# PEER channel mixer: another order for the low halves, the one-hot pairs and the packed operands on VectorE and ScalarE

## The reference

```python
q = (xb @ w_q).reshape(P_BLOCK, P_HEADS, P_QDIM)
s1, s2 = q[..., :128] @ k1.T, q[..., 128:] @ k2.T      # 128 keys each
v1, i1 = lax.top_k(s1, 16);  v2, i2 = lax.top_k(s2, 16)
cand = v1[..., :, None] + v2[..., None, :]
top_s, pos = lax.top_k(cand, 16)                       # 16 of 256 pairs, 8 heads
eid = take(i1 * 128 + i2, pos);  gate = softmax(top_s)
act = gelu(einsum(u_tab[eid], xb))                     # exact GELU
out = einsum(gate * act, v_tab[eid])
```

## Time and profile before

| | us |
|---|---|
| runs, median of 3 | 1959.04 |
| profiled execution, its own time | 1959.04 |
| its span, first to last instruction | 1957.3 |
| TensorE busy | 1925.2 (98%) |
| VectorE busy | 1430.1 (73%) |
| ScalarE busy | 1183.5 (60%) |
| GpSimd busy | 237.9 (12%) |
| mean granted TensorE clock | 0.999 of full speed |

### The profile page before, as it was taken

One profiled execution on the slowest core, in us unless ns is written; L12 is line 12 of the kernel. 1 busy time (PEld: TensorE's weight loads), 2 busy tenths in 40 slices (PEclk: granted clock), 3 DMA queues, 4 the chain that ended last, 5 costly groups with the idle time before them and its releaser, 6 DMA issues.

```text
span 1957.3 us, 40098 instructions
## 1 busy us (share of the span) xinstructions
PE 1925.2 (98%) x13148; PEld 1747.0 (89%) x13148; DVE 1430.1 (73%) x2525; ACT 1183.5 (60%) x1610; POOL 237.9 (12%) x106
## 2 busy tenths in 40 slices
PE   8989999999999999999999999999999999999998
PEld 6878999999999888888888799999999998888887
DVE  4775896889898666666658669868989876666666
ACT  4534446888887455555565544568888865555554
POOL 0113743000000000000006067310000000000000
PEclk9999999999999999999999999999999999999999
DMA  7744455444445555555554345554444455555554
GB/s 250 244 139 158 157 191 174 151 150 150 153 152 164 197 193 193 193 193 192 193 162 139 129 148 167 180 167 154 153 150 150 152 182 193 193 193 193 193 193 150
DMA packets 92817, 338.97 MB, mean 173 GB/s; under 512 B 10384, under 2 KB 10512, under 8 KB 92240
## 3 DMA queue, kind: packets, MB, share of 16 engines
q1 hardware_dynamic: 90864, 329.49, 51.3%
q0 software_dynamic: 1888, 8.62, 1.4%
HBM read 337.02 MB, written 1.05 MB: 173 GB/s over the span
## 4 chain that ended last, share of the span: by engine, by line
PE 88%; issue 3%; DVE 3%; POOL 3%; ACT 1%; DMA 0%; SPq 0%; POOLq 0%; DVEq 0%; ACTq 0%
PE psum L1132 88%; POOL tile_lo L386 3%; DVE tile_lo L726 1%; ACT tile_hi L457 1%; DMA raw<-in_a_in 0%; DVE zv L827 0%; DVE qe L1070 0%; DVE zu L836 0%; DVE ke L1071 0%; ACT hT_hi L492 0%; DVE zu L801 0%; DVE hn L776 0%; DVE score_in L1082 0%; DVE x L760 0%; DVE yT_lo L842 0%
## 5 line engine op out<-in xcount | busy, mean ns | idle before, releaser
L726 DVE TENSOR_TENSOR tile_lo<-raw,tile_hi 128x1024 fp32r<-128x1024 f32 x564 | 696.2, 1234 | 282.7 <-ACT tile_hi L457 282.3
L457 ACT ACTIVATE tile_hi<-raw 128x1024 fp32r<-128x1024 f32 x624 | 655.8, 1052 | 270.6 <-PE psum L1132 268.2
L1132 PE MATMUL psum<-hT_hi,tile_hi 128*128 128x256 f32 x2368 | 595.6, 290 | 3.4 <-ACT hT_hi L492 2.7
L1132 PE MATMUL psum<-hT_lo,tile_hi 128*128 128x256 f32 x2368 | 577.6, 283 | 0.0
L1132 PEld LDWEIGHTS psum<-hT_hi,tile_hi 128*128 128x128 f32 x2368 | 451.2, 191 | 7.9 <-ACT hT_hi L492 3.4
L1132 PEld LDWEIGHTS psum<-hT_lo,tile_hi 128*128 128x128 f32 x2368 | 452.3, 192 | 0.0
L1132 PE MATMUL psum<-hT_hi,tile_lo 128*128 128x256 f32 x2368 | 332.1, 283 | 0.5 <-POOL tile_lo L386 0.5
L597 ACT ACTIVATE w_hi<-acts 128x256 fp32r (+1 forms) x256 | 106.7, 418 | 340.8 <-PE psum L1132 340.8
L1132 PEld LDWEIGHTS psum<-hT_hi,tile_lo 128*128 128x128 f32 x2368 | 305.4, 192 | 1.2 <-POOL tile_lo L386 0.9
L1132 PE MATMUL psum<-tile_lo,w_hi 128*128 128x512 f32 x1024 | 274.9, 389 | 0.0
L1132 PE MATMUL psum<-tile_hi,w_lo 128*128 128x512 f32 x1024 | 274.7, 389 | 0.0
(11 more groups left out here) (194 smaller groups left out, 1479.3 us busy)
## 6 DMA issues: line engine op xcount, KB each, us to landing
raw<-in_u SPq DMA_DIRECT2D x256, 512.0 KB, 3.4
raw<-in_v SPq DMA_DIRECT2D x256, 512.0 KB, 3.4
raw<-in_a_in SPq DMA_DIRECT2D x32, 512.0 KB, 4.7
raw<-in_w_q SPq DMA_DIRECT2D x32, 512.0 KB, 3.4
raw<-in_a_out SPq DMA_DIRECT2D x16, 512.0 KB, 3.4
raw<-in_b_rv SPq DMA_DIRECT2D x16, 512.0 KB, 3.4
raw<-in_b_qk SPq DMA_DIRECT2D x8, 512.0 KB, 3.4
raw<-in_b_out SPq DMA_DIRECT2D x8, 512.0 KB, 3.4
```

The lines of the kernel that those rows point to most:

```text
L457: act.activation(tile_hi[slot % SPLIT_SLOTS][:, :], raw[slot][:, :], ACT.Copy).then_inc(hi_ready, 1)
L726: dve.tensor_tensor(tile_lo[s][:, :], raw[slot][:, :], tile_hi[s][:, :].bitcast(F32), ALU.subtract).then_inc(lo_ready, 1)
L1132: return pe.matmul(o, a, b, start=start, stop=stop, skip_group_check=True)
```

## The change

The lookup on VectorE writes its lower halves at other places; the one-hot pairs of the first two groups begin later and only two groups are packed before the late tiles; in each late tile VectorE runs the gate, the one-hot pair, the lower half, the product and then the weighting, where it ran pair, gate, weighting, lower half and product; and ScalarE packs group g + 2 in the tile of group g and waits for the weighted copies before both of its two instructions.

```diff
@@ ScalarE
-                def pack_group(slot, hot, ready, used):
-                    act.wait_ge(hot_ready[l], hot)
+                def pack_group(slot, ready, used):
+                    act.wait_ge(weighted_ready[l], ready)
                     if used is not None:
                         act.wait_ge(gmat_done[l], used)
                     act.activation(pack[:, slot, 0, ...], hot_a ...)
-                    act.wait_ge(weighted_ready[l], ready)
                     act.activation(pack[:, slot, 1:4, ...], weighted ...)
...
-                early_tiles(EARLY - 4, EARLY - 2)
-                pack_group(0, 1, 1, None)
-                early_tiles(EARLY - 2, EARLY - 1)
-                pack_group(1, 3, 2, None)
-                early_tiles(EARLY - 1, EARLY)
+                early_tiles(EARLY - 4, EARLY - 3)
+                pack_group(0, 1, None)
+                early_tiles(EARLY - 3, EARLY - 2)
+                pack_group(1, 2, None)
+                early_tiles(EARLY - 2, EARLY)
                 act.wait_ge(w16_ready[l], 1)
-                pack_group(0, 5, 3, 1)
...
-                    if more:
-                        g = next_group(c) + 2
+                    if more and c in GROUP_AT:
+                        g = GROUP_AT.index(c) + 2
@@ VectorE, lookup
                 n = UT[l] + POOL_U
+                lo_at(n)
...
+                lo_at(n + 1)
+                n += 2
...
                         d2 = did(dve.tensor_tensor(look ... ALU.mult))
-                        lo_at(n)
-                        n += 1
+                        if h == 0:
+                            lo_at(n)
+                            n += 1
...
-                    if half == 0:
-                        lo_at(n)
-                        n += 1
...
-                for k in range(EXP_AT + 2, TURN_AT + 3):
-                    lo_at(UT[l] + k)
+                first_onehots = EARLY - RAW_SLOTS
+                with dve.Fori(0, (first_onehots - EXP_AT) // RAW_SLOTS) as i:
+                    for c in range(RAW_SLOTS):
+                        lo_in(i, c, UT[l] + 2 + EXP_AT)
...
@@ VectorE, late tile
-                    if more:
-                        hot_pair(token2, g % 2, ...)
                     if g is not None:
                         if not (first and c < 2):
                             dve.wait_ge(late_gated[l], i * LATE_STEP + (c - 1))
                         gate(...)
-                    if more:
-                        weigh(token2, ...)
+                        if more:
+                            hot_pair(token2, g % 2, ...)
                     lo(n % RAW_SLOTS, ...)
                     ... late_product(i, c - 1, ...)
+                    if more:
+                        weigh(token2, ...)
@@ VectorE, first groups
                 dve.wait_ge(picksT_ready[l], 3)
+                hot_pair(0, 0, None)
                 rest = did(dve.tensor_tensor(gelu_out[:, 0, :], psum[:, 5, 0:T], w16[:, 0, :], ALU.subtract))
-                lo_at(UT[l] + TURN_AT + 3)
+                lo_at(UT[l] + first_onehots + 2)
                 after(rest)
                 rest = did(dve.tensor_copy(w16[:, 1, :], gelu_out[:, 0, :]))
-                hot_pair(0, 0, None, None)
...
-                lo_at(UT[l] + TURN_AT + 4)
                 dve.wait_ge(w16_ready[l], 1)
                 weigh(0, 2, None)
-                lo_at(UT[l] + TURN_AT + 5)
-                hot_pair(GROUP, 1, 1, None)
-                lo_at(UT[l] + TURN_AT + 6)
-                lo_at(UT[l] + EARLY - 1)
+                lo_at(UT[l] + first_onehots + 3)
+                hot_pair(GROUP, 1, 1)
                 weigh(GROUP, 4, 2)
                 lo_at(UT[l] + EARLY)
```

More of the change, by code:

```diff
@@ L588, in late_tile @@
                     hi(n % RAW_SLOTS, i * (LATE_STEP // RAW_SLOTS * 16) + 16 * (n // RAW_SLOTS + 1), t + (n - 1))
-                    if more:
-                        g = next_group(c) + 2
-                        pack_group(g % 2, i * (2 * STEP_GROUPS) + (2 * g + 1), i * STEP_GROUPS + (g + 1), i * STEP_GROUPS + (g - 1))
+                    if more and c in GROUP_AT:
+                        g = GROUP_AT.index(c) + 2
+                        pack_group(g % 2, i * STEP_GROUPS + (g + 1), i * STEP_GROUPS + (g - 1))
                 def gated_hi(k, slot, used):
@@ L603, in early_tiles @@
                         act.activation(acts[:, k, :], psum[:, k % 4, 0:T], ACT.Gelu).then_inc(gelu_done[l], 1)
-                early_tiles(EARLY - 4, EARLY - 2)
-                pack_group(0, 1, 1, None)
-                early_tiles(EARLY - 2, EARLY - 1)
-                pack_group(1, 3, 2, None)
-                early_tiles(EARLY - 1, EARLY)
-                act.wait_ge(w16_ready[l], 1)
-                pack_group(0, 5, 3, 1)
[L613 to L617, removed]
+                early_tiles(EARLY - 4, EARLY - 3)
[3 more added lines that the diff above has]
+                early_tiles(EARLY - 2, EARLY)
+                act.wait_ge(w16_ready[l], 1)
                 for c in range(LATE_STEP):
-                    late_tile(0, c, next_group(c) is not None)
+                    late_tile(0, c, True)
                 with act.Fori(1, LATE_STEPS - 1) as i:
                     for c in range(LATE_STEP):
-                        late_tile(i, c, next_group(c) is not None)
+                        late_tile(i, c, True)
                 for c in range(LATE_STEP):
@@ L628, in peer @@
                         gated_hi(1, 1, None)
-                    g = next_group(c)
-                    late_tile(LATE_STEPS - 1, c, g is not None and (LATE_STEPS - 1) * STEP_GROUPS + g + 2 < GROUPS)
+                    g = GROUP_AT.index(c) + 2 if c in GROUP_AT else GROUPS
+                    late_tile(LATE_STEPS - 1, c, (LATE_STEPS - 1) * STEP_GROUPS + g < GROUPS)
                 act.wait_ge(late_gated[l], N_LATE)
@@ L900, in peer @@
                 d2 = did(dve.scalar_tensor_tensor(pos_b[:, :, :], place, float(WIDE_ROWS * TOPK), part1[:, :, :], ALU.is_lt, ALU.mult))
+                lo_at(n + 1)
+                n += 2
                 after(d2)
-                did(dve.tensor_tensor(pos_b[:, :, :], pos_b[:, :, :], part2[:, :, :], ALU.add))
+                d2 = did(dve.tensor_tensor(pos_b[:, :, :], pos_b[:, :, :], part2[:, :, :], ALU.add))
                 d2 = did(dve.tensor_copy(rank16[:, :, :], iota[:, 0:TOPK].unsqueeze(2).broadcast_to([P, TOPK, TOPK])))
-                after(d2)
                 for half, pos in ((0, pos_a), (1, pos_b)):
+                    if half == 0:
+                        after(d2)
+                    else:
+                        dve.wait_ge(looked[l], 1)
                     numbers = topi16[:, :, :, :].rearrange("p h (g s) r -> p (h g) s r", s=2)[:, :, half, :]
@@ L908, in peer @@
                     ranks = rank16[:, :, :].unsqueeze(1).broadcast_to(full)
-                    if half == 1:
-                        dve.wait_ge(looked[l], 1)
                     eqs = []
@@ L947, in peer, with hot_pair @@
                                       ALU.mult).then_inc(gates_ready[l], 1)
-                for k in range(EXP_AT + 2, TURN_AT + 3):
-                    lo_at(UT[l] + k)
-                def hot_pair(token0, slot, weighed, read):
-                    if weighed is not None:
-                        dve.wait_ge(weighted_ready[l], weighed)
+                first_onehots = EARLY - RAW_SLOTS
+                with dve.Fori(0, (first_onehots - EXP_AT) // RAW_SLOTS) as i:
+                    for c in range(RAW_SLOTS):
+                        lo_in(i, c, UT[l] + 2 + EXP_AT)
+                def hot_pair(token0, slot, read):
                     if read is not None:
-                        dve.wait_ge(packed[l], read)
+                        dve.wait_ge(weighted_ready[l], read)
                     for numbers, out in ((picks_a, hot_a[:, slot, :, :]), (picks_b, hot_b[:, :, :])):
@@ L990, in late_tile @@
                     token2 = None if g is None else i * (STEP_GROUPS * GROUP) + (g + 2) * GROUP
-                    if more:
-                        hot_pair(token2, g % 2, i * STEP_GROUPS + (g + 2), i * (2 * STEP_GROUPS) + 2 * (g + 1))
                     if g is not None:
@@ L996, in late_tile @@
                         gate(i * (STEP_GROUPS * GROUP) + g * GROUP, 4 + g % GATE_BANKS, i * STEP_GROUPS + (g + 1))
-                    if more:
-                        weigh(token2, i * (2 * STEP_GROUPS) + 2 * (g + 3), i * (2 * STEP_GROUPS) + 2 * (g + 2))
+                        if more:
+                            hot_pair(token2, g % 2, i * STEP_GROUPS + (g + 2))
                     n = UT[l] + 1 + EARLY + c
@@ L1003, in late_tile @@
                         late_product(i, c - 1, min(gates, GROUPS) if last else gates)
+                    if more:
+                        weigh(token2, i * (2 * STEP_GROUPS) + 2 * (g + 3), i * (2 * STEP_GROUPS) + 2 * (g + 2))
                 dve.wait_ge(picksT_ready[l], 3)
+                hot_pair(0, 0, None)
```

(10 more changed lines are left out.)

## The result

| | before | after |
|---|---|---|
| runs, median (before: the three above and a fourth) | 1959.11 us | 1977.27 us (1975.89 to 1978.81) |
| profiled execution, its own time | 1959.04 | 1976.48 |
| its span | 1957.3 | 1974.5 |
| TensorE busy | 1925.2 | 1929.2 |

What follows compares the result with a forecast made beforehand. TensorE was taken as the bound; 2.2 (lookup) + 4.9 (first groups) + 1.5 (late tiles) = 8.6 us per layer, 17.2 for two layers, moving the span from 1957.3 to 1974.5 and the time to 1976 us, range 1968 to 1984.

Steps and rivals of the forecast that it cites:

- lookup, net: Lookup: TensorE waits for the lower halves of tiles 22 and 25, less 0.2 lost before: +2.2 us per layer.
- tile 39: First groups: TensorE waits for the upper half of tile 39, queued behind ScalarE's packs: 1.71 + 0.11 us.
- tile 40: First groups: after the gate matrices TensorE waits for the upper half of tile 40: 2.45 us.
- third group's pack: After tile 40: the third group, no longer packed ahead, has its pack ready late for TensorE: 0.6 us.
- late loop, net: Late tiles: late packs cost 3.8 us, tiles without gates win back 2.3: net +1.5 us per layer.
- the undisturbed short instructions: Lookup, VectorE: all six run after GpSimd's last lower half, undisturbed, in about 1.75 us.
- Rival C: Lookup: the short instructions stay slow, 3.9 us a layer more, 1984 us; chance 8%.
- Rival B: Late loop doesn't hold its 0.5 us of slack: 0.3 more at each of 2 x 20 places, 1988 us; chance 10%.
- Rival A: Late tiles and first groups: ScalarE's relief decides, stalls hidden, 5.0 us faster, 1954 us; chance 4%.

Runs made afterwards that it cites:

- the lookup alone: The kernel before with only the changed kernel's lookup on VectorE: 1963.44 us, ratio 1.0026.
- its front alone: The kernel before with only the lower halves of tiles 16 and 17 moved as in the change, other lookup places kept: 1958.49 us, ratio 0.9997.
- the wait filled: The changed kernel with 36 matmuls of 128 columns on constants between the first gate matrices and tile 40: 1974.35 us.
- the first attempt: The late order alone, with ScalarE's pack before the upper half in tiles c = 0 and 4, third group's pair and weighting before the first gate: 2010.17 us.
- the second attempt: The first attempt with VectorE's weighting right behind the one-hot pair in tiles c = 0 and c = 4: 1953.13 us, ratio 0.9969.
- its variant: The second attempt with ScalarE's pack ahead of the GELU in tiles c = 0 and c = 4: 1953.43 us, ratio 0.9972.
- the late order alone: The changed kernel with the lookup and the first two groups' places as in the kernel before: 1962.04 us, ratio 1.0018.
- ScalarE's order changed back: The changed kernel with ScalarE packing groups 0 and 1 one tile later in its queue, as in the kernel before: 1966.34 us.

## Why the prediction was right, point by point

Measured are starts of the last 8 matmuls of tiles in layer 0, each less its start at the pace of 2.88 or 3.61 us. From tile 16 to tile 127 it is 379.0 us (271.61 to 650.63) where it was 370.0 (272.75 to 642.74). In layer 1 it is 378.9 where it was 370.0, so the two layers make 17.9 us. Tile 16 of layer 0 itself came 1.1 us earlier than before, in a part that the change doesn't touch; without that the span would have grown by 18.3, which is close to what the medians show (18.2).

| per layer, us | predicted | measured |
|---|---|---|
| lookup, net | +2.2 | +2.4 |
| tile 39 | 1.8 | 1.8 |
| tile 40 | 2.45 | 4.0 |
| third group's pack | 0.65 | 0.1 |
| late loop, net | +1.5 | +0.8 |
| sum (rows rounded) | 8.6 | 9.0 |

- **Lookup: right.** lo(21) to lo(22) 3.92 predicted and 3.91 measured; stalls of 0.96 and 1.43 predicted, 1.08 and 1.57 measured with their restarts (3.87 + 2.97 and 4.35 + 2.98, each less 2 x 2.88). Both halves of the mechanism are shown: the missing places by the lookup alone against its front alone, the undisturbed short instructions by the rows (1.74 us for the six, 1.75 predicted). Rival C fell with them.
- **Tiles 39 and 40: the mechanism right, the term for tile 40 too small.** The wait itself was as predicted: 2.50 us, from 343.97 + 0.65 = 344.62 to 347.12, where I had 2.45. The step that failed is the price of tile 40 behind it, whose 16 matmuls I took at full clock, 2.00 us; they ran at 1.2 GHz and took 3.49 (347.12 to 350.61), 1.5 us more per layer. With the wait filled they took 1.98 (347.13 to 349.11).
- **Third group: too large, for the same reason.** The slow tile 40 gave ScalarE and VectorE that time; with the wait filled the loss is 0.51 again. The error at tile 40 (+1.5) is mostly offset by this one (-0.5) and by that of the late loop (-0.7), so the closeness of the total is in good part luck.
- **Late loop: right in kind, 0.7 too high.** Packs come 0.13 and 0.21 late in each 8 tiles and 0.11 comes back in each tile without gates: 27.78 us per 8 tiles against 27.65. The nine steps from tile 48 to tile 120 cost 1.2 in this way, where my +0.16 a step makes 1.4. At the ends the loop gains, which I hadn't counted: the first tile without gates took 3.16 us before and takes 2.88 now, and the last 7 tiles, with few packs left, take 0.1 less than before.
- **Rival B** didn't come true in the changed kernel, but a loop of its kind is real: the first attempt walked into one, with the lower half as a further link, at 25 us a layer over the kernel before.
- **Rival A** named the right gain: ScalarE's lag, priced at 2.3 us per layer, cost the kernel before 2.4 in the rows. The gain came without the stalls only in the second attempt and its variant.

## What to carry to other kernels

When several in-order queues feed a busy engine, read for every operand when it is ready and when it is wanted; the sum of the differences gave this change to within 1.3 us (in part by luck, as said), where the list of waits of the kernel before was all but empty. An instruction that waits delays all that stands behind it, so put what the busy engine wants next ahead of it, and follow the chain through the other engines until it closes: one swap on ScalarE cost some 51 us (ratio 1.0278 against 1.0018), and with the third group prepared early and the weighting moved on VectorE as well the same swap gave a kernel 6 us under before. Idle time of a side engine costs nothing in itself; missing places for its due work do.

## What the runs showed of the hardware that I had not expected

TensorE's clock fell to 1.2 GHz after a wait of 2.30 us that followed one of 1.52 us, with 24 + 12 matmuls between them. The slow time was some 3.4 us in layer 0 and began 1.3 us after the restart in layer 1, at about the same total loss (tiles 40 and 41 together come 4.0 us late in both). 36 small matmuls in the wait, 2.17 us of them, kept it at 2.4 GHz.

The kernel before has such a fall too, in the mixer between the two stretches, and it comes and goes. There TensorE waits 1.94 or 1.95 us for VectorE (`bo`) in every kernel. In seven of the eleven profiled executions, of the kernel before and of the changed one among them, the clock falls behind that wait; in the other four (the filled wait, the late order alone, the second attempt and its variant) the same wait leaves it at 1.00. The kernel before, then the second attempt:

```profile
1100.00:1102.00 2.00, 2.00 (x8) 1.58 (x8) 1.96 (x4) 1.19 (x2) 0.00 (x0) 0.50 0.00 0
1098.00:1100.00 2.00, 1.36 (x6) 0.80 (x6) 1.57 (x3) 0.53 (x1) 0.00 (x0) 1.00 0.00 0
```

From tile 127 of layer 0 to tile 16 of layer 1 it takes 588.4 us in three profiled executions without this fall (the filled wait, the late order alone, the second attempt), and with it 588.6 in the kernel before, 588.7 with ScalarE's order changed back and 589.1 in the changed kernel. This is where the 0.7 us between the changed kernel and the one with the filled wait come from. What decides whether it falls there no run shows.
